# Operand sums of the first MLP moved from VectorE to accumulating DMAs, and the modulation products reordered

## The reference, cut to what matters

```python
for i in range(DEPTH):                       # DEPTH = 2
    mod_l = silu(c) @ ada_w[i] + ada_b[i]    # 6 vectors of 1024: shift, scale, gate, twice
    mod_c = silu(c_ctx) @ ada_w[i] + ada_b[i]
    ...                                      # mixer, x = LN(alpha*x + g1*y)
    h = x * (1.0 + s2) + sh2
    x = LN(alpha*x + g2 * (square(relu(h @ w1)) @ w2))   # w1: 1024x4096, w2: 4096x1024
```

## Time and the profile before

| | us |
|---|---|
| median of 3 runs | 1975.93 (1973.90 to 1977.81) |
| the profiled execution, own time | 1977.81 |
| its span in the trace | 1976.0 |
| PE busy | 1951.7 (99% of the span) |
| DVE busy | 1321.2 (67%) |
| ACT busy | 642.5 (33%) |
| POOL busy | 402.7 (20%) |

### The profile page before, as it was taken

The page is one execution under the profiler, slowest core; times in us unless marked ns, Lnnn a source line. Parts: engine busy times, 40 slices in busy tenths (PEclk is TensorE's granted clock), DMA queues, the critical chain, the costliest instruction groups (busy, mean ns, idle before and its releaser), DMA issues.

```text
span 1976.0 us, 25032 instructions
## 1 busy us (share of the span) xinstructions
PE 1951.7 (99%) x9525; PEld 1671.2 (85%) x9525; DVE 1321.2 (67%) x1886; ACT 642.5 (33%) x894; POOL 402.7 (20%) x372
## 2 busy tenths in 40 slices
PE   9999999998899999999999999999999999999998
PEld 6889889888789988888888888888888888888887
DVE  4756678689787777767774553553554477777778
ACT  3413222234323222322534223323323334444443
POOL 0300311325312222222350020020020026200004
PEclk9999999999999999999999999999999999999999
DMA  9613334236798999999322131222122125877656
GB/s 339 242 64 75 115 120 137 93 102 151 164 245 217 224 228 245 237 236 247 112 76 75 43 102 59 70 75 70 65 68 87 54 85 171 228 216 194 176 146 149
DMA packets 112742, 286.66 MB, mean 145 GB/s; under 512 B 16368, under 2 KB 29296, under 8 KB 112496
## 3 DMA queue, kind: packets, MB, share of 16 engines
q1 hardware_dynamic: 86400, 223.02, 33.7%
q0 software_dynamic: 24400, 58.21, 17.0%
q10 hardware_dynamic: 1824, 3.85, 0.6%
HBM read 238.34 MB, written 2.12 MB: 122 GB/s over the span
## 4 chain that ended last, share of the span: by engine, by line
PE 89%; issue 3%; POOL 3%; DVE 2%; DMA 2%; ACT 1%; SPq 0%; POOLq 0%; DVEq 0%; ACTq 0%
PE bank L1000 16%; PE bank L1002 16%; PE bank L1001 16%; PE bank L1038 7%; PE bank L1040 7%; PE bank L1039 7%; PE bank L1401 3%; PE bank L1404 3%; PE bank L1403 3%; PE bank L1606 2%; PE bank L1603 2%; PE bank L1605 2%; PE bank L1308 1%; PE bank L1357 1%; POOL res_lat L3065 1%
## 5 line engine op out<-in xcount | busy, mean ns | idle before, releaser
L2101 DVE TENSOR_TENSOR w_lo<-raw,w_hi 128x1024 fp32r<-128x1024 f32 x132 | 174.9, 1325 | 243.5 <-ACT w_hi L1629 243.2
L1629 ACT ACTIVATE w_hi<-raw 128x1024 fp32r<-128x1024 f32 x132 | 139.4, 1056 | 371.8 <-PE bank L1040 199.1
L1038 PE MATMUL bank<-w_hi,hT_hi 128*128 128x512 f32 x592 | 230.6, 390 | 0.0
L1039 PE MATMUL bank<-w_lo,hT_hi 128*128 128x512 f32 x592 | 230.4, 389 | 0.0
L1040 PE MATMUL bank<-w_hi,hT_lo 128*128 128x512 f32 x592 | 230.4, 389 | 0.0
L1000 PE MATMUL bank<-w_hi,act_hi 128*128 128x512 f32 x504 | 198.7, 394 | 1.4 <-DVE w_lo L2101 1.3
L1000 PE MATMUL bank<-hT_hi,w_hi 128*128 128x384 f32 (+2 forms) x544 | 193.1, 355 | 4.9 <-ACT rbuf L1937 4.9
L1002 PE MATMUL bank<-w_hi,act_lo 128*128 128x512 f32 x504 | 196.5, 390 | 0.0
L1001 PE MATMUL bank<-w_lo,act_hi 128*128 128x512 f32 x504 | 196.3, 389 | 0.0
L1001 PE MATMUL bank<-hT_lo,w_hi 128*128 128x384 f32 (+2 forms) x544 | 191.6, 352 | 0.0
L1002 PE MATMUL bank<-hT_hi,w_lo 128*128 128x384 f32 (+2 forms) x544 | 191.6, 352 | 0.0
(11 more groups left out here) (389 smaller groups left out, 4359.7 us busy)
## 6 DMA issues: line engine op xcount, KB each, us to landing
raw<-w_units_d SPq DMA_DIRECT2D x242, 512.0 KB, 3.7
wsum<-w_units_d SPq DMA_DIRECT2D x52, 512.0 KB, 5.0
mod<-mod_units_d SPq DMA_DIRECT2D x64, 384.0 KB, 5.8
wsum<-w_units_d POOLq DMA_DIRECT2D x26, 512.0 KB, 7.9
wsum<-wsum POOLq DMA_DIRECT2D x26, 512.0 KB, 6.2
bv<-mod_units_d SPq DMA_DIRECT2D x16, 512.0 KB, 3.5
mod<-mod_units_d SPq DMA_DIRECT2D x14, 512.0 KB, 7.9
res_lat<-rbuf POOLq DMA_DIRECT2D x28, 256.0 KB, 5.5
```

The source lines that it names most:

```text
L1038: nc.tensor.matmul(bank[t][:, :], hT_hi[:, kc, tt], hi[:, c], start=kc == 0, stop=False)
L1039: nc.tensor.matmul(bank[t][:, :], hT_hi[:, kc, tt], lo[:, c], start=False, stop=False)
L1629: nc.scalar.activation(halves_of(phase, k, i)[0], raw[:, s, :], ACT.Copy).then_inc(hi_done, 1)
L2101: tt(lo, raw[:, s, :], f32(hi), ALU.subtract).then_inc(lo_done, 1)
```

## The change

It has two parts.

The first concerns the operand sums in `ffn0a`. The three `whole_operand` additions and the two additions of `s4` leave DVE's list. Instead ACT copies `hT_hi` into `x21`, `x22`, `x11` at the end of chunk 1, and POOL issues two accumulating DMAs per block (`add_operand`) that add `hT_lo`, after `ln_scale_shift`. For `s4`, four such DMAs add `hT_hi` and `hT_lo` to `x22`, two before and two after the first round of `add0`. The weight sums T1 and T2 move behind these DMAs from between the scaling steps, their slots are renumbered, and SP loads T1's block only after all six bias DMAs have landed. DVE waits for the three blocks at the end of chunk 2.

The second concerns the modulation products. Group 7 is spread over pieces 3 to 5 (two, three, three products), and group 6 stands alone in `ffn0z`, with two products at each of places 0 to 3. Groups 3 to 6 share one accumulator. The extra places between the drains of a piece are gone.

```diff
 MOD1_SEQ = [(g, n) for g in range(PIECES_MIXED) for n in range(KC)]
-MOD1_SEQ += [(g, n) for g in range(PIECES_MIXED, PIECES_F) for n in range(KC)]
-MOD1_PLACES = [[1, 1, 2, 2, 2]] * 3 + [[1, 2, 2, 2, 3], [2, 2, 2, 2, 3], [2, 2, 2, 2, 3, 3], [2, 3]]
+for _p, _a, _b in ((3, 0, 2), (4, 2, 5), (5, 5, 8)):
+    MOD1_SEQ += [(_p, n) for n in range(KC)] + [(7, n) for n in range(_a, _b)]
+MOD1_SEQ += [(6, n) for n in range(KC)]
+MOD1_PLACES = [[1, 1, 2, 2, 2]] * 3 + [[1, 2, 2, 2, 3]] + [[1, 2, 2, 3, 3]] * 2 + [[2, 2, 2, 2]]
...
-        SLOT0 = {T1: 1, T2: 2, T3: 0, T4: 1}
+        SLOT0 = {T1: 0, T2: 1, T3: 2, T4: 0}
...
-            load_base0(0, T1)
-            load_base0(0, T2)
             for k in range(RAW):
                 weights(at + k)
+            load_base0(0, T3)
+            load_base0(0, T2)
+            sp.wait_ge(shifted0, 16 * TILES0)
+            load_base0(0, T1)
...
-            sp.wait_ge(shifted0, 16 * TILES0)
-            load_base0(0, T3)
             mods1(0)
             mods1(1)
...
+                    if phase == "ffn0a" and c == 1:
+                        for dst, k, t in ((x21, first, t_second), (x22, second, t_second), (x11, first, t_first)):
+                            nc.scalar.activation(dst[:, :, :], hT_hi[:, k, t].bitcast(F32), ACT.Copy).then_inc(x_copied, 1)
...
-                    operand0_hi(4, x22, s4_hi[:, :, :])
                     block0_hi(0, 0)
+                    act.wait_ge(s4_whole, 64)
+                    nc.scalar.activation(s4_hi[:, :, :], x22[:, :, :], ACT.Copy).then_inc(s_hi0, 1)
...
-                    if phase == "ffn0a":
-                        if c == 0:
-                            dve.wait_ge(stage_lo, before("stage", "ffn0a"))
-                            whole_operand(x11, first, t_first)
-                        if c == 1:
-                            dve.wait_ge(pe_step, step_of("ffn0a", 0, "up1.1"))
-                            whole_operand(x21, first, t_second)
-                            whole_operand(x22, second, t_second)
-                        if c == 2:
-
-                            dve.wait_ge(x_whole, 3)
-                            operand0_sum(1, x22, x21, x22)
-                            operand0_sum(2, x21, x11, x21)
+                    if phase == "ffn0a" and c == 2:
+
+                        for n in range(3):
+                            dve.wait_ge(x_whole[n], 32)
+                        operand0_sum(1, x22, x21, x22)
+                        operand0_sum(2, x21, x11, x21)
...
-                    tt(x22[:, :, :], x22[:, :, :], f32(hT_hi[:, second, t_first]), ALU.add).then_inc(x_whole, 1)
                     for t in range(TILES0):
                         drain0(-1, 0, t)
                     split_lo(phase, i, 7)
-                    dve.wait_ge(x_whole, 4)
-                    tt(x22[:, :, :], x22[:, :, :], f32(hT_lo[:, second, t_first]), ALU.add).then_inc(s_sum0, 1)
...
-                    if t in (0, 3):
-                        weight_sum0(0, (T1, T2)[t // 3])
+            def add_operand(dst, src, k, t, whole):
+
+                for h in range(2):
+                    part = slice(k.start + 2 * h, k.start + 2 * h + 2)
+                    nc.gpsimd.dma_start(dst[:, 2 * h:2 * h + 2, :], src[:, part, t].bitcast(F32), accum_op=ALU.add).then_inc(whole, 16)
...
             ln_scale_shift()
-            weight_sum0(0, T3)
+            for n, (dst, k, t) in enumerate(((x21, first, t_second), (x22, second, t_second), (x11, first, t_first))):
+                pool.wait_ge(x_copied, n + 1)
+                add_operand(dst, hT_lo, k, t, x_whole[n])
+            for x in (T3, T1, T2):
+                weight_sum0(0, x)
             pool.wait_ge(shifted0, 16 * TILES0)
+
+            pool.wait_ge(s_lo0, 3)
+            add_operand(x22, hT_hi, second, t_first, s4_whole)
             add0(-1, 0)
+            pool.wait_ge(s4_whole, 32)
+            add_operand(x22, hT_lo, second, t_first, s4_whole)
             add0(-1, 1)
```

More of the change, by code:

```diff
@@ L434, in build @@
         gy_added = [sem(f"gy_added{t}") for t in range(TILES0)]
-        x_whole = sem("x_whole")
+        x_copied = sem("x_copied")
+        x_whole = [sem(f"x_whole{x}") for x in range(3)]
         s_sum0 = sem("s_sum0")
@@ L438, in build @@
         s_lo0 = sem("s_lo0")
+        s4_whole = sem("s4_whole")
         shifted0 = sem("shifted0")
@@ L589, in block0_used @@
             return step_of("ffn0a", 0, UNIT_END["ffn0a"][6 + n])
-        def sum1(g, v=0):
-            return macc[:, v if g < PIECES_MIXED else (g - PIECES_MIXED) % 2, :]
         def up_block(p, x):
@@ L912, in piece_loads @@
                 mods(4)
-                mods(5)
             for p in range(PIECES_F - 1):
@@ L1409, in rows @@
                     pe.wait_ge(mod_used, len(MOD1_SEQ) if phase == "ffn0z" else MOD1_SEQ.index((p, KC - 1)) + 1)
-                    mod_sums(phase, i, "rows0", 6, [sum1(p), sum1(PIECES_F - 1 if phase == "ffn0z" else p, 1)],
+                    mod_sums(phase, i, "rows0", 6, [macc[:, 0, :], macc[:, 0 if PIECES_MIXED <= p < PIECES_F - 2 else 1, :]],
                              WIDE_M1 // 2)
@@ L2250, in done, with products @@
                     dve.wait_ge(dve_drain, drained(phase, i, f"q{q}.{j}")[1])
-                def products(place, at=None):
-                    here = places[place] if place < len(places) else ()
-                    for n in here if at is None else here[at:at + 1]:
+                def products(place):
+                    for n in places[place]:
                         mod_product(n)
@@ L2343, in ffn0 @@
                         drain0(p, 1, t)
-                        if t < TILES0 - 1:
-                            products(5, t - 2)
                     block0_lo(p + 1, 1)
@@ L2772, in mod_product @@
                 elif g:
-                    dve.wait_ge(pe_step, step_of("ffn0", g - 1 if g <= PIECES_MIXED else g - 2, "rows0"))
+                    dve.wait_ge(pe_step, step_of("ffn0", g - 1 if g < 7 else PIECES_MIXED - 1, "rows0"))
                 unit = mod1[:, n % SLOTS_M1, :]
                 for v in reversed(range(2 if g < PIECES_MIXED else 1)):
-                    acc = sum1(g, v)
+                    acc = macc[:, 1 if g == 7 else v, :]
                     if kc == 0:
@@ L2803, in gate_unit @@
                     .then_inc(gated, 1)
-            def whole_operand(out, k, t):
-                tt(out[:, :, :], f32(hT_hi[:, k, t]), f32(hT_lo[:, k, t]), ALU.add).then_inc(x_whole, 1)
             def operand0_sum(n, out, a, b):
@@ L3094, in ln_scale, with ln_scale_shift @@
                         gt(res(t)[:, c], res(t)[:, c], lnbc[:, 0, c], ALU.mult).then_inc(res_mul, 1)
+            def ln_scale_shift():
+                pool.wait_ge(lnbc_scaled, 1)
+                pool.wait_ge(stage_lo, before("stage", "ln0a") + 2 * KC)
+                for t in range(TILES0):
+                    for h in range(2):
+                        c = slice(h * 512, (h + 1) * 512)
+                        gt(res(t)[:, c], res(t)[:, c], lnbc0[:, 0, c], ALU.mult).then_inc(res_mul, 1)
+                    pool.wait_ge(res_mul, BASE_MUL["ln0a"] + 2 * t + 2)
+                    nc.gpsimd.dma_start(res(t), lnbc0[:, 1, :], accum_op=ALU.add).then_inc(shifted0, 16)
             def weight_sum0(p, x):
```

## The result

| | before | after |
|---|---|---|
| median, us | 1976.84 (1973.90 to 1977.81, 4 runs) | 2025.16 (2023.84 to 2025.53, 4 runs) |
| span of the profiled execution | 1976.0 | 2023.1 |

The changed kernel is slower by 48.3 us: ratio 1.0246, 95% interval 1.0228 to 1.0264. Forecast were 2020 us with a range from 1988 to 2038, and 2003 to 2041 for the likeliest case alone.

The account below looks back on a forecast made before the run. PE, busy 99% of the span, was taken as the bound, so any wait is lost in full. +37.1 at q6, -1.8 in pieces 4 and 5, +8.5 in `ffn0z` made +43.8 us on 1977.8, median forecast 2020, range 1988 to 2038.

Parts of the forecast that it names:

- Rival (a): On POOL's queue: two operand DMAs go together, X about 510.5, q6 at 550.4; +17 us, 1993 us; chance 0.20.
- Rival (b): On POOL's queue: only bytes bind, X 506, q6 at 545.9; +12.6 us, 1989 us; chance 0.07.
- Rival (c): In `ffn0a`: adds hidden, DVE's freed 8.6 us removes PE's waits and two restarts; -7.8 us, 1968 us; chance 0.05.
- X: Time when the three blocks in `ffn0a` are whole, after six serial operand DMAs; 524.7 us, bounds 518.7 to 534.9.
- Rival (d): In `ffn0z`: PE's wait doesn't come, all else does; 2011 us; chance 0.66 shared with the main forecast.
- When the first operand DMA goes out: On POOL in `ffn0a`: last bias DMA near 488, first operand DMA near 490.2 us, when that has landed.
- The time of one DMA: On POOL's queue: 5.5 us per 384 KB operand DMA plus 0.25 to the next issue; six taken as serial.
- From X to PE: In `ffn0a`: PE resumes its down product 8.9 us after X, at 533.6 instead of 506.4.
- From X to q6: In `ffn0a`: `s4` through POOL's queue puts q6 at X + 52.4, 577.1 instead of 540.0; +37.1 us.
- The relu drains and `up3.0`: In `ffn0a`: ACT's copies (4.2 us) less DVE's relief (3) start `up3.0` about 1 us later than 486.5.
- Pieces 4 and 5: One product at place 0 instead of two removes PE's waits of 1.5 and 0.3 us; -1.8 us, low bound 0.
- `ffn0z`: Four products behind the last result make PE wait 6.3 us at `rows`, plus a 2.2 us restart; +8.5 us.

Follow-up runs that it names:

- e3: Changed kernel with each operand block added by four DMAs of 128 rows instead of two of 256; 2015.63 us.
- e10: Changed kernel with each block's two operand DMAs issued behind the scaling of tiles 3, 4 and 5 instead of after all six; 2015.72 us.
- e2: Kernel before with only the second part of the change, the new modulation product order; 1979.94 us against 1976.22, ratio 1.0020.
- e11: Changed kernel with SP loading the blocks of T3 and T2 only after all six bias DMAs have landed; 2021.96 us.
- e5: e1 with `s4` summed on DVE as before, so only the three blocks come by DMA; 2004.45 us.
- e1: Kernel before with only the first part of the change, the operand sums by copies and accumulating DMAs; 2018.4 us.
- e8: Kernel before with one product at place 0 of pieces 4 and 5 instead of two, moved to the last places; 1975.16 us beside 1974.76.
- e9: e7 with the product places of e8 for pieces 4 and 5 added; 1970.90 us against 1977.08, ratio 0.9963.
- e7: Kernel before with SP loading T3's block ahead of two unit loads instead of behind them; 1971.14 us against 1977.08, ratio 0.9965.

## Why the prediction was right, point by point

**The mechanism** held in each step: operand DMAs one at a time, DVE standing at them, PE at DVE; then `s4` through the same queue and a second wait before q6; a third at `rows`. Rival (a) fell: no two operand DMAs went together, and e3 and e10 show what does. Rival (b) fell: the queue's engines were busy for 47.2% only. Rival (c) fell with X at 531.88 where 493.4 was the balance. Rival (d) fell in the trace of the changed kernel and in e2.

**When the first operand DMA goes out** was the term most off: 490.2 forecast, 501.0 measured, 10.8 us late. The step "the last bias DMA goes out near 488" took POOL's rhythm of 3.7 us from the rows and left out two pauses of the queue, 5.80 us before 487.49 and 5.09 before 501.0. The kernel before showed such a pause already, 4.67 us before 489.43. e11 shows that a part of the first is SP's loads, a side of the change that the prediction left without a price.

**The time of one DMA** was 4.7 us from issue to issue, not 5.75, for all but the first, which needed 7.6 beside 1.05 MB of SP's loads. Six took 30.9 us instead of 34.5. Together X = 531.9 instead of 524.7, +7.2, inside the bounds of 518.7 to 534.9. That is partly luck: the two errors have opposite signs. With its own 5.75 us and the start that was measured, X would have been 535.5, outside these bounds. The lower bound of q6, 564, does not come out of the terms either: ten DMAs of 1 us less give 567. And the two restarts of rival (c) are 4.4 us, not 4.0; neither changes the forecast.

**From X to PE** was given as 8.9 us and took 8.97. **From X to q6** it was 52.4 and took 51.6: T3, T1 and T2 landed 6.4, 13.2 and 19.4 us behind X and the two `hT_lo` adds of `s4` 42.3 and 47.0, all within 1.1 us of the forecast. So q6 came 43.4 us later than before instead of 37.1, all from X. The waits were 38.1 and 11.3 us, forecast 27 and 12. The restart behind q6 was taken to be the same in both kernels, and is not quite. The first 8 us behind q6 in the changed kernel, against the rows from 540.00 in the earlier trace rows and from 544.00 in the kernel before (third row here):

```profile
583.40:587.40 4.00, 3.97 (x14) 3.97 (x15) 1.17 (x2) 0.00 (x0) 1.13 (x2) 0.58 1.06 210
587.40:591.40 4.00, 4.00 (x25) 4.00 (x24) 2.92 (x5) 1.06 (x1) 0.00 (x0) 1.00 1.07 292
...
544.00:548.00 4.00, 4.00 (x21) 4.00 (x21) 2.19 (x5) 1.06 (x1) 0.00 (x0) 0.86 0.94 225
```

The clock came back to 1.00 sooner, and by the 16th matmul behind q6 the changed kernel had made up 0.7 us.

**The relu drains and `up3.0`.** Forecast was about 1 us later. The drain row stands at 483.88, before at 485.90, and the wait at `up3.0` fell from 4.9 to 2.4 us: sign wrong, size small, and it disappears in what follows. DVE's relief was bigger than the 3 us allowed against ACT's 4.2: 6.2 us, as the drains came 2.0 us earlier in spite of the copies. The low part that took 4.44 us in the earlier trace rows now took 1.21, no longer under a whole pair of POOL's multiplications:

```profile
474.00 1.21 DVE L2104 TENSOR_TENSOR w_lo<-raw,w_hi 128x1024 fp32r<-128x1024 f32 x1
```

**Pieces 4 and 5.** Their waits are gone. From q6 to `rows` 3.3 us were gained besides the new wait, where 1.8 were forecast. With the matmuls of both traces side by side, 0.7 of them are the shorter restart behind q6, 2.0 lie at the wait of piece 4 and 0.6 at that of piece 5. The waits themselves were 1.8. That the product at place 0 causes them is shown in part: every kernel with part 2 has none, but with the products as before they also shrink to 0.6 us in e5 and 0.9 in e1, and the places alone (e8, e9) remove the one of piece 4 and leave one in piece 5.

**`ffn0z`.** The wait was 5.9, forecast 6.3. The restart came. Against the kernel before, 1.1 us of its 2.2 show at the end of the span (1.4 in e2 up to the next layer); against e1, which has no restart and hardly a wait behind `rows`, it is 2.5. So the size was about right, and the comparison with the kernel before is smaller because that kernel had 1.0 us of waits of its own there.

The sum was +43.8 and came to +47.1 in the spans: +6.3 at q6, -1.5 between (the restart behind q6 and the pieces), -0.4 at the wait, -1.1 at the restart.

## What to carry to other kernels

Moving five additions (8.6 us of DVE) to accumulating DMAs replaced them with ten DMAs of which no two go together, 4.4 us each when alone and up to 9.3 beside other transfers, at a place where DVE, ACT and PE all wait for them in order. Price a move onto a queue by when the queue is free and by how many rows it lets in flight, not by bytes, and look for "issue" pauses of the issuing engine at that place in the old trace. When you read off what a clock restart costs, compare with a kernel that has no waits of its own behind that place. Where a transfer is late, first ask whether its load stands needlessly behind others: that swap (e7, and e9 with it) was the only thing here that made the kernel faster, by 0.35%.

## What was not expected of the hardware

- POOL's queue let three DMAs of 144 packets go together, or one of 272 with one of 144, but never two of 272. What sets this limit was not tested. With one in flight at a time its engines were busy for 53.0% of the 4.6 us.
- An accumulating DMA from SBUF to SBUF of 384 KB in rows of 1.5 KB lands after 4.4 us when alone, and after 7.3 us (changed kernel) and 9.6 us (e11) beside SP's loads.
- After three 144-packet bias DMAs POOL paused until the third had landed, although two were done; this was seen in the kernel before, the changed one, and e11. Its cause is open.
